# Differential attention: ScalarE copies a unit's second group of turned rows ahead of both exponentials of the step

## What is computed

```
for i in range(S // Q_BLOCK):               # 8 blocks of 128 queries
    qb, kb, vb = q[:, q0:kend], k[:, :kend], v[:, :kend]     # keys up to the block
    s = einsum('bqhjd,bkhjd->bhjqk', qb, kb) * scale         # j = 0, 1: two maps
    s = s - slopes * dist
    s = where(dist >= 0, s, -inf)
    p = softmax(s, axis=-1)
    a = p[:, :, 0] - lam * p[:, :, 1]
    outs.append(einsum('bhqk,bkhe->bqhe', a, vb))
```

## Time and profile before

| | |
|---|---|
| median of 3 runs | 3343.8 us (3342.38 to 3344.1) |
| the profiled execution | 3344.28 us, its span 3342.4 us |
| TensorE matmul busy | 3271.5 us, 98% of the span |
| VectorE busy | 2132.6 us, 64% |
| GpSimd busy | 1503.2 us, 45% |
| ScalarE busy | 1149.6 us, 34% |
| mean granted TensorE clock | 0.994 |

### The profile page before, as it was taken

How to read it: one execution, slowest core, us unless ns; L and a number is a source line. 1 busy time by engine, 2 the same in 40 slices (tenths; PEclk the granted TensorE clock), 3 DMA queues, 4 the chain that set the end, 5 groups by cost and what they waited for, 6 DMA issues and landing times. The chain is left out here.

```text
span 3342.4 us, 43883 instructions
## 1 busy us (share of the span) xinstructions
PE 3271.5 (98%) x17076; PEld 2680.6 (80%) x17076; DVE 2132.6 (64%) x3009; ACT 1149.6 (34%) x2094; POOL 1503.2 (45%) x967
## 2 busy tenths in 40 slices
PE   8999999999999999999999999999999999999997
PEld 7778778878778888777888888889887778888886
DVE  5777645777647233878667685631458776676656
ACT  2230352130353001565333344510027543333454
POOL 4535324535414433326565554443332375655443
PEclk9999999999999999999999999999999999999998
DMA  4112103112101111103223354311120122223642
GB/s 159 39 34 86 60 20 92 47 33 81 66 14 45 57 39 39 51 9 119 103 95 109 109 217 164 117 44 58 32 70 7 66 99 107 101 99 127 238 155 88
DMA packets 98883, 275.17 MB, mean 82 GB/s; under 512 B 22912, under 2 KB 23296, under 8 KB 89216
## 3 DMA queue, kind: packets, MB, share of 16 engines
q1 hardware_dynamic: 76448, 241.20, 20.7%
q10 hardware_dynamic: 22240, 31.27, 2.9%
HBM read 214.24 MB, written 58.98 MB: 82 GB/s over the span
## 5 line engine op out<-in xcount | busy, mean ns | idle before, releaser
L1433 PE MATMUL ps<-sl_r,sl_r 128*128 128x512 f32 x5544 | 1265.9, 390 | 6.4 <-DVE sl_r L2667 3.4
L1433 PEld LDWEIGHTS ps<-sl_r,sl_r 128*128 128x128 f32 x5544 | 1041.9, 188 | 229.1 <-DVE sl_r L2667 5.0
L751 POOL TENSOR_TENSOR w_hi<-w_raw,ones_r 128x512 fp32r<-128x512 f32 x220 | 282.4, 1284 | 860.9 <-PE ps L954 844.6
L954 PE MATMUL ps<-in_hi,w_hi 128*128 128x512 f32 x1920 | 613.8, 401 | 15.6 <-DVE in_lo L2038 10.0
L954 PE MATMUL ps<-in_hi,w_lo 128*128 128x512 f32 x1920 | 598.7, 393 | 0.0
L954 PE MATMUL ps<-in_lo,w_hi 128*128 128x512 f32 x1920 | 598.0, 393 | 0.0
L954 PEld LDWEIGHTS ps<-in_hi,w_hi 128*128 128x128 f32 x1920 | 347.9, 189 | 102.5 <-issue 34.8
L954 PEld LDWEIGHTS ps<-in_lo,w_hi 128*128 128x128 f32 x1920 | 358.8, 188 | 76.4 <-issue 1.4
L954 PEld LDWEIGHTS ps<-in_hi,w_lo 128*128 128x128 f32 x1920 | 357.6, 188 | 75.2 <-issue 1.4
L844 POOL TENSOR_TENSOR sl_r<-sl,sl_r 128x1024 fp32r<-128x1024 f32 x92 | 249.3, 2722 | 313.0 <-ACT sl_r L1811 300.2
L754 POOL TENSOR_TENSOR w_lo<-w_raw,w_hi 128x512 fp32r<-128x512 f32 x220 | 337.0, 1532 | 17.3
(11 more groups left out here) (247 smaller groups left out, 4328.8 us busy)
## 6 DMA issues: line engine op xcount, KB each, us to landing
w_raw<-w_in SPq DMA_DIRECT2D x136, 512.0 KB, 3.3
raw_pair<-w_ffn SPq DMA_DIRECT2D x68, 1024.0 KB, 5.4
sl<-op_kept SPq DMA_DIRECT2D x70, 512.0 KB, 5.1
op_kept<-sl SPq DMA_DIRECT2D x44, 512.0 KB, 2.9
op_kept<-st SPq DMA_DIRECT2D x22, 512.0 KB, 2.7
x_put_away<-xt SPq DMA_DIRECT2D x16, 512.0 KB, 7.8
xt<-x_put_away SPq DMA_DIRECT2D x16, 512.0 KB, 10.1
op_kept<-st SPq DMA_DIRECT2D x22, 256.0 KB, 2.0
```

The source lines that it names most:

```text
L751: pool.tensor_tensor(w_hi[:, j, cols], w_raw[:, j, cols], ones[:, 0:1].broadcast_to([P, HALF]), ALU.mult).then_inc(pool_own, 1)
L954: last = pe.matmul(ps[:, (2 * j if bank is None else bank) + h, :], w[:, w_slot, (w_k + k) * P:(w_k + k + 1) * P], part[:, k0 + k, h * HAL ...
L1433: last = pe.matmul(ps[:, to[name], :], ring(sl_r, p, wp[w])[:, k * P:(k + 1) * P], part, start=(name in ("P1", "P5") and k == 0 and wp is ...
```

## The change

In ScalarE's steps the second copy moves ahead of both exponentials. `exps` loses its argument `between`.

```diff
-                def exps(u, between=None):
+                def exps(u):
...
                     for j in range(maps):
                         m = maps * u + j
-                        if j and between:
-                            between()
-
                         lane = j if maps == 2 else t % 2
...
+                    if kind == "dif" and 3 <= u < len(units) + 3:
+                        groups(u - 3, 1)
                     if kind == "dif" and 1 <= u < len(units) + 1:
-                        exps(u - 1, (lambda: groups(u - 3, 1)) if u >= 3 else None)
-                    elif kind == "dif" and 3 <= u < len(units) + 3:
-                        groups(u - 3, 1)
+                        exps(u - 1)
```

## The result

| | before | after |
|---|---|---|
| median | 3343.77 us (3342.38 to 3344.10, 9 runs) | 3353.86 us (3352.22 to 3357.48, 9 runs) |
| the profiled execution, its span | 3344.28, 3342.4 us | 3356.24, 3354.3 us |

The ratio is 1.0033, with a 95% interval of 1.0025 to 1.0041: slower, by 10.1 us. I had forecast 3350.8 and given 3346.5 to 3355.0.

The account below looks back on a forecast made before the run. TensorE was taken to bound the stage, busy 68.56 of 74.00 us. 3.45 - 0.53 + 0.6 = 3.5 us a layer, 7.0 for two, on the median 3343.8 gave 3350.8 us, range 3346.5 to 3355.

Parts of the forecast that it names:

- term A: Steps after heads: the first exponential loses its cover under ScalarE's wait, delaying the next first copy; +3.45 us a layer.
- E0: The first of ScalarE's two exponentials in a step; 0.92, 1.03 or 1.13 us for 768, 896 or 1024 columns.
- T1: TensorE's turn into bank 6 that feeds ScalarE's copy of a unit's second group.
- C1: ScalarE's copy of a unit's second group; in ordinary steps forecast to start no earlier than 0.53 us after T1 starts.
- Term B: Crowded steps after heads: the second copy passes an exponential it had stood behind; -0.53 us a layer.
- Term C: VectorE's mix and score reductions: second exponential ends later, so TensorE's scores wait; +0.6 us a layer, bounds 0 to 1.4.
- E1: The second of ScalarE's two exponentials in a step; forecast to end 2.8 to 3.1 us after T1 starts.
- C0: ScalarE's copy of a unit's first group; forecast to have no slack in four steps per layer, those after heads.
- Rival 1: VectorE takes over: TensorE's scores wait 0.2 us in 12 steps, 3355.6 us in all; chance 0.15.
- Rival 3: Part is won back as later TensorE waits shorten, term A and Term C halved: 3347.3 us; chance 0.10.
- rival 4: TensorE's pauses, soon about 1.5 us, lower its clock to the 1.2 GHz level; above 3356 us; chance under 0.02.
- Rival 2: Not slower: in steps after heads, slack behind the first copy leaves only Term B, 3342.7 us; chance 0.06.

Follow-up runs that it names:

- old_in_head_steps: The changed kernel with the old order kept in the steps that end with the heads' copy and squares; 3345.06 us, ratio 1.0008 to the kernel before.
- short_mix: The changed kernel with VectorE's mix run only over the first tile in rounds 4 to 7; 3354.38 us, ratio 1.0031 to the kernel before.
- deferred_squares_and_last_heads: Kernel before, heads' squares (rounds 3-5) one step later, step 31's heads copy ahead of second exponential, squares after step 32's first copy, step 32 new order; 3340.57 us.

## Why the prediction was right, and where it was off

**Direction and term A: right.** The five lines of A were forecast at 3.45 us a layer and measured 3.55, each within 0.1 (step 33: +0.14 for +0.06). old_in_head_steps shows that they come from the head steps: E0 used to run while ScalarE waited for T1, and lost that cover. That C1 could start no earlier is the row pair of u = 25, 1.17 us in both kernels. The waits did not all stand where I had put them, at T1: in step 24 they are 0.28 before the weighing and 0.45 before T1, and in step 32 all 2.02 us stand before the weighing, which waits for the heads copy.

**Term B: a little too large,** -0.39 for -0.53. In u = 24 T1 now comes out of a wait, its row is 0.55 long and not the 0.49 of u = 25 from which I took 1.17, C1 starts 0.58 behind it (1436.99) and T0 follows 1.22 after T1, where I had 1.17.

**Term C: mis-sized, and with the wrong cause on top.** Forecast 0.6 with bounds of 0 and 1.4, measured 1.67 a layer, outside the bounds. I traced E1 to the mix to the scores, which is real (0.35, 0.16 and 0.28 us where it stands alone, close to my 0.28, 0.12 and 0.20). The step that failed is the sentence that outside the head steps "the same sum without heads is at most 4.0, under TensorE's own 4.4 to 5.0, so C0 is in time". C0 was in time for T1. In steps 23, 27 and 31 the turn back needs it earlier, and I did not trace E1 to C0 to the turn back. These are the two rows in the timeline of the kernel before:

```profile
1427.15 0.48 ACT L1556 ACTIVATE st<-ps 128x384 f32<-128x384 f32 x1
...
1428.19 0.66 PE L1172 MATMUL ps<-ident,rfac 128*128 128x128 f32 x4
```

They are 1.04 apart. After the change they are 0.62 apart (1428.77 and 1429.39), and 0.62 in short_mix too, where the row shows TensorE held for this copy (0.44). So there were 0.4 us of room, and a second exponential of 0.9 in front of the copy used them up. My own terms had it: from T1 of 22, 0.42 + 0.27 + 1.84 to C0 and 0.62 to the turn back make 3.15, before 2.65, so +0.5 for a measured +0.48 in step 23. This one term is 2.1 of the 3.1 us between forecast and median. That the total still fell into the range is in part luck: the range had its width from rivals 1 and 3, not from this wait.

**The clock: rival 4 had under 0.02, and its mechanism is there, its size is not.** It predicted more than 3356 us. The profiled execution took 3356.24 with one fall in it, but the median is 3353.86. I had argued that the clock survived today's pauses. Inside the two stretches these were 0.9 us, and my own terms implied about 2.0 (1.1 us of added work in front of the heads copy) where I had written 1.5. And outside them the trace of the kernel before had the case already, 71 us behind the first stretch, where 1.49 us of pause (after three of 0.57 to 0.73) are followed by the half clock:

```profile
1555.21 3.01 PE L1003 MATMUL ps<-ones_r,st 128*128 128x1 f32 x16 [1.49 <-DVE st L2048]
...
1554.00:1560.00 6.00, 4.79 (x21) 4.44 (x22) 6.00 (x9) 0.20 (x1) 2.16 (x1) 0.65 0.01 3
```

For the mechanism the chance was too low. A fall at step 32 costs 0.6 to 1.3 us, and its share of the median is small beside C.

**Rival 1** asked for waits for VectorE in 12 steps. The loads of the scores waited for it 4 times, 1.3 us in all (3 times and 0.5 us in before), and partly under another wait. **Rival 2** falls with the wait of 0.45 at T1 of 24. **Rival 3**, part won back, falls too: 10.1 us measured for the 9.8 that two layers lose. One reading was narrow without harm: the 2.8 to 3.1 us from T1 to the end of E1 hold for groups of three tiles, and the same terms give 2.3 for u = 20 and 3.4 for u = 31.

**The advice of the Trainium skill.** The wait of 0.21 before T0 recurs in every ordinary step, and the rule of the Trainium skill, Perfetto Trace Analysis, section Optimization Strategy, to make what a gap waits for start sooner, picked this target. In this case, outside the crowded steps, the copy already started as soon as its own input allowed, and the rule's gain is the 0.4 us of B. deferred_squares_and_last_heads follows the same rule with C0 and the heads copy, which had stood behind other work of ScalarE, and gains 1.4 a layer.

## What to carry to other kernels

Before you move an instruction up on an in-order engine, look at whether its input is there at the new place. If it is not, the move only takes the cover off what it passed, and each thing behind it gets later: walk to every reader of those, not only the one you have in mind. Where a step loses time, take each possible wait away alone and then both, since a wait that shows in the trace may have a second one beneath it. And where an engine waits for another, look at what that other engine waited for some steps earlier: the delay of step 23 began in step 21.

## What the runs showed of the hardware

At step 32 TensorE's clock fell to its 1.2 GHz level at a single pause of 2.0 to 2.2 us in 8 of 16 layers, and in none of 12 layers with a pause of at most 0.9 us. The half clock began between 0.5 us ahead of the pause's end and 1.3 us behind it, stood for about 3.4 us in all eight, and cost 0.6 to 1.3 us (S of the two layers of one kernel). The same kernel shows it in one layer and not in the next, and in one execution and not in another. What decides it at this size of pause stays open.

The half clock also follows shorter pauses. Some 74 us behind T1 of 34, in every kernel and both layers, TensorE pauses a few times for 0.5 to 0.75 us and then once for 1.47 to 1.50 us, before 16 matmuls of one column each (L1003). Of these 28 passages in the 14 profiles the clock stayed up in 5, stood at the half level for about 3.4 us in 9, and for about 6.8 us in 14. After the second layer these falls go with the times. From T1 of 34 to the end of the span it is 723.7 to 724.0 us in the three profiles without a fall there, 725.0 to 725.1 in the four with 3.4 us of it, and 726.2 to 726.9 in the seven with 6.8. The two profiled executions of the changed kernel differ by 2.3 us there (726.2 and 723.9), and by 1.1 us in S of the first layer. So the larger part of this scatter comes from a place that the change does not touch.
